# Scores of the short-range heads: even and odd heads in one step of 24 matmul instructions on four PSUM banks, alternating between the row halves of the array

## The reference

```python
def swa_sink_attention(q, k, v, positions, rel_bias, sinks):
    nb = S // BLOCK                                    # 256 // 128 = 2
    q = q.reshape(B, nb, BLOCK, SWA_KV_HEADS, SWA_GROUP, SWA_HEAD_DIM)     # 2 groups of 8 heads, 64 wide
    k_band = _band(k...); v_band = _band(v...)         # the block before and this block
    s = jnp.einsum('bnqhgd,bnkhd->bnhgqk', q, k_band).astype(jnp.float32) * (SWA_HEAD_DIM ** -0.5)
    s = s + bias                                       # relative bias of each head
    s = jnp.where(valid, s, -jnp.inf)                  # 0 <= distance < 128
    m = jnp.maximum(jnp.max(s, axis=-1, keepdims=True), sink)
    e = jnp.exp(s - m)
    p = e / (jnp.sum(e, axis=-1, keepdims=True) + jnp.exp(sink - m))
    out = jnp.einsum('bnhgqk,bnkhd->bnqhgd', p, v_band)
```

## Time and profile before

| | us |
|---|---|
| median of 3 runs | 2618.0 |
| lowest and highest | 2617.82, 2619.82 |
| profiled execution | 2617.56 |
| its span, first to last instruction | 2615.8 |
| PE busy | 2586.5 (99%) |
| DVE busy | 1652.0 (63%) |
| ACT busy | 1374.8 (53%) |

### The profile page before, as it was taken

How to read it: one execution, slowest core, us unless ns; L and a number is a source line. 1 busy time by engine, 2 the same in 40 slices (tenths; PEclk the granted TensorE clock), 3 DMA queues, 4 the chain that set the end, 5 groups by cost and what they waited for, 6 DMA issues and landing times.

```text
span 2615.8 us, 32927 instructions
## 1 busy us (share of the span) xinstructions
PE 2586.5 (99%) x13278; PEld 2179.5 (83%) x13278; DVE 1652.0 (63%) x2064; ACT 1374.8 (53%) x2013; POOL 0.2 (0%) x4
## 2 busy tenths in 40 slices
PE   9999999999999999999999999999999999999998
PEld 7877888888888888887888888888888888888887
DVE  7685566555655567568788866544566555655556
ACT  5664454444444446568878845544444444444444
POOL 0000000000000000000000000000000000000000
PEclk9999999999999999999999999999999999999999
DMA  6533565566556655555454437544565556555554
GB/s 224 165 134 137 195 208 193 193 192 187 189 189 193 193 190 168 190 178 176 137 179 145 131 128 249 164 158 138 184 206 186 188 193 193 193 188 190 189 190 145
DMA packets 235534, 468.78 MB, mean 179 GB/s; under 512 B 8219, under 2 KB 17654, under 8 KB 234102
## 3 DMA queue, kind: packets, MB, share of 16 engines
q1 hardware_dynamic: 234246, 465.11, 54.9%
q10 hardware_dynamic: 1136, 1.58, 0.2%
HBM read 460.36 MB, written 6.29 MB: 178 GB/s over the span
## 4 chain that ended last, share of the span: by engine, by line
PE 49%; DVE 1%; issue 0%; ACT 0%; DVEq 0%; ACTq 0%
PE ps L1176 10%; PE ps L1178 10%; PE ps L1177 10%; PE ps L1215 9%; PE ps L1214 5%; PE ps L1570 1%; PE ps L1583 1%; PE ps L1712 1%; PE ps L1687 1%; PE ps L1550 0%; PE ps L1233 0%; DVE AC L2965 0%; PE ps L1535 0%; PE ps L1609 0%; PE ps L1623 0%
## 5 line engine op out<-in xcount | busy, mean ns | idle before, releaser
L2483 DVE TENSOR_TENSOR WL<-Wt,WH 128x1024 fp32r<-128x1024 f32 (+1 forms) x861 | 1040.8, 1210 | 810.1 <-ACT WH L1767 750.1
L1767 ACT ACTIVATE WH<-Wt 128x1024 fp32r<-128x1024 f32 (+1 forms) x861 | 899.0, 1047 | 882.7 <-PE ps L1178 532.3
L1176 PE MATMUL ps<-WH,XT 128*128 128x512 f32 (+1 forms) x1184 | 472.1, 399 | 1.9 <-DVE Um L2875 1.6
L1176 PE MATMUL ps<-WH,HT 128*128 128x512 f32 (+2 forms) x1176 | 458.1, 390 | 4.5 <-DVE WL L2483 3.3
L1178 PE MATMUL ps<-WH,XT 128*128 128x512 f32 (+1 forms) x1184 | 459.5, 388 | 0.0
L1177 PE MATMUL ps<-WL,XT 128*128 128x512 f32 (+1 forms) x1184 | 458.6, 387 | 0.0
L1178 PE MATMUL ps<-WH,HT 128*128 128x512 f32 (+2 forms) x1176 | 451.7, 384 | 0.0
L1177 PE MATMUL ps<-WL,HT 128*128 128x512 f32 (+2 forms) x1176 | 451.2, 384 | 0.0
L1215 PE MATMUL ps<-XT,WH 128*128 128x512 f32 x960 | 336.5, 394 | 0.0
L1215 PE MATMUL ps<-HT,WH 128*128 128x512 f32 x960 | 336.5, 394 | 0.0
L1214 PE MATMUL ps<-XT,WL 128*128 128x256 f32 x960 | 266.6, 278 | 0.0
(11 more groups left out here) (390 smaller groups left out, 1965.8 us busy)
## 6 DMA issues: line engine op xcount, KB each, us to landing
Wt<-in_mlp_w SPq DMA_DIRECT2D x128, 1024.0 KB, 5.2
Wt<-in_w_up SPq DMA_DIRECT2D x64, 1024.0 KB, 5.5
Wt<-in_w_down SPq DMA_DIRECT2D x64, 1024.0 KB, 5.0
Wt<-in_w_in SPq DMA_DIRECT2D x53, 1024.0 KB, 5.1
Wt<-in_w_out SPq DMA_DIRECT2D x32, 1024.0 KB, 5.1
Wt<-in_xa_wk SPq DMA_DIRECT2D x16, 1024.0 KB, 5.1
Wt<-in_xa_wv SPq DMA_DIRECT2D x16, 1024.0 KB, 5.1
Wt<-in_xa_wq SPq DMA_DIRECT2D x16, 1024.0 KB, 5.1
```

What stands on the lines that cost most here:

```text
L1176: pe.matmul(o, xh, wh, start=start, stop=False)
L1767: act.activation(m.WH[:, i % NR, 0:2 * w], m.Wt[:, slot % NW, h * 2 * w:(h + 1) * 2 * w], ACT.Copy).then_inc(*up("wsplit.a", i))
L2483: dve.tensor_tensor(m.WL[:, i % NR, 0:2 * w], m.Wt[:, slot % NW, h * 2 * w:(h + 1) * 2 * w], m.WH[:, i % NR, 0:2 * w].bitcast(F32), SUB).t ...
```

## The change

The two scores steps of a group become one. It takes four banks from the queue at once and makes all 12 matmuls (24 instructions on PE), one for the even head and one for the odd head in turn, each pair on the two row halves and in different banks. One semaphore stands at their end. ACT then copies two banks instead of one. The mask steps of even and odd heads both come after the next half, with the first maximum. One `yield` less stands in each group, so each later step of a group comes one half earlier, and the next group of the same generator too: nine halves instead of ten. In `rope_products` a wait on the keys' transposition becomes one on the sums of the product before it.

```diff
-        def scores(hg, odd):
-            b = [p.bank(), p.bank()]
-            p.do("swa_scores", par, hg, odd, *b)
+        for hg in (par, par + 2):
+            b = [p.bank() for _ in range(4)]
+            p.do("swa_scores", par, hg, *b)
             p.free(b[0])
-            return b
-
-        for hg in (par, par + 2):
-            b = scores(hg, 0)
-            yield
-            p.do("swa_masked", par, hg, 0, b[1])
-            p.free(b[1])
-            b = scores(hg, 1)
-            yield
-            p.do("swa_masked", par, hg, 1, b[1])
-            p.free(b[1])
+            p.free(b[2])
+            yield
+            for odd in range(2):
+                p.do("swa_masked", par, hg, odd, b[2 * odd + 1])
+                p.free(b[2 * odd + 1])
             p.do("swa_largest", par, hg, 0)
             yield
             p.do("swa_largest", par, hg, 1)
...
     @named
-    def swa_scores(par, hg, odd, b0, b1):
-        k0, k1 = m.bank(b0), m.bank(b1)
+    def swa_scores(par, hg, *bs):
         g = hg // 2
         on.wait_ge(*at("swa.a", "keys"))
-        for s in freed(b0) + freed(b1):
-            on.wait_ge(*s)
+        for b in bs:
+            for s in freed(b):
+                on.wait_ge(*s)
         for i in range(2):
-            pb, tile = odd * 64, 2 * hg + i
+            tile = 2 * hg + i
             on.wait_ge(*at("swa.a", "queries", tile // 2))
-            q0 = m.QST[pb:pb + 64, tile, :]
-            kk = m.KTD[pb:pb + 64, g, :]
-            for o, qs, ks in ((k0[:, 2 * i * P:(2 * i + 1) * P], 0, 0),
-                              (k0[:, (2 * i + 1) * P:(2 * i + 2) * P], 1, 0),
-                              (k1[:, i * P:(i + 1) * P], 1, 1)):
-                t = pe.matmul(o, q0[:, qs * P:(qs + 1) * P], kk[:, ks * P:(ks + 1) * P], start=True, stop=True)
-        t.then_inc(*up(f"swa{par}.t", "scores", hg, odd))
+            for k, qs, ks in ((0, 0, 0), (0, 1, 0), (1, 1, 1)):
+                for odd in range(2):
+                    rows = slice(odd * 64, odd * 64 + 64)
+                    n = i if k else 2 * i + qs
+                    t = pe.matmul(m.bank(bs[2 * odd + k])[:, n * P:(n + 1) * P], m.QST[rows, tile, qs * P:(qs + 1) * P],
+                                  m.KTD[rows, g, ks * P:(ks + 1) * P], start=True, stop=True)
+        t.then_inc(*up(f"swa{par}.t", "scores", hg))
...
     @named
-    def swa_scores(par, hg, odd, b0, b1):
+    def swa_scores(par, hg, *bs):
         st = f"swa{par}"
-        on.wait_ge(*at(st + ".t", "scores", hg, odd))
+        on.wait_ge(*at(st + ".t", "scores", hg))
         swa_spare()
         if hg >= 2:
             on.wait_ge(*at(st + ".t", "turn", hg - 2, 1))
-        act.activation(m.S[:, par, odd, :, :, :].rearrange("p i b k -> p (i b k)"), m.bank(b0), ACT.Copy).then_inc(
-            *up(st + ".a", "scores", hg, odd, frees=b0))
+        for odd in range(2):
+            act.activation(m.S[:, par, odd, :, :, :].rearrange("p i b k -> p (i b k)"), m.bank(bs[2 * odd]), ACT.Copy
+                           ).then_inc(*up(st + ".a", "scores", hg, odd, frees=bs[2 * odd]))
...
-            on.wait_ge(*at("rope.v", "kt"))
+            on.wait_ge(*(at("rope.v", c - 1) if c else at("rope.v", "kt")))
```

## The result

| | before | after |
|---|---|---|
| median, us | 2618.0 | 2623.0 |
| profiled execution | 2617.56 | 2622.36 |
| its span | 2615.8 | 2620.6 |

The changed kernel takes 2622.95 us, the kernel before beside it on the same chip 2617.99, so 5.0 us more: ratio 1.0018, 95% interval 1.0011 to 1.0025. The forecast was +2.5.

What follows compares the result with a forecast made beforehand. PE was taken as the bound, with the chain through ACT and DVE already holding it up at three points. Scores -6.4 and waits +9.3 gave +2.9, taken as +2.5: 2618.0 + 2.5 = 2620.5 us, range 2611 to 2625.

Steps and rivals of the forecast that it cites:

- Scores: Short-range scores on PE: row halves overlap, four merged steps of 1.62 us replace eight, -6.4 us.
- Waits: PE's waits for the short-range chain after the steps move earlier: 14.0 us against 4.7, so +9.3 us.
- value 0: Group 0's value step, after half 40: PE waits 3.3 us for DVE to take out the turned probabilities.
- scores 2: Group 2's scores, after half 41: norm_turn took the only idle bank, four are wanted; PE waits 2.2 us.
- value 2: Group 2's value step, after half 49: DVE works without pause, turned probabilities come late; PE waits 3.3 us.
- DVE's idle time: Behind the PE wait at scores 2, through score copies and a split on ACT: DVE idle some 3.8 us.
- The clock: PE's granted clock in the short-range stretch: no wait of 1.6 us had lowered it; nothing in the sum.
- rival (d): Waits grow, or PE's clock falls after one (one half at 1.2 GHz costs 2.7): 2624 to 2626 us; chance 0.07.
- 200 to 203: Sign of being right: first matmul of w_out on XT starts at 200 to 203 us; account put it at 201.5.
- Rival (a): ACT and DVE keep up, 6.6 us of value waits and half the bank waits hidden: 2610 to 2612; chance 0.15.
- Rival (c): In the short-range stretch half of the waits go: -2 us, 2616; chance 0.11.
- Rival (b): Row halves don't overlap, merged scores step 2.95 us instead of 1.62: 2623.5, at most 2626; chance 0.13.

Runs made afterwards that it cites:

- run 1: Changed kernel with one more yield between turn and value of each group: 2616.59 us against 2618.79 for the kernel before.
- run 6: Kernel before with its steps moved as in the change, scores not merged, even step then odd step: 2623.82 us against 2618.22 for the kernel before.
- run 2: Changed kernel with three unread 512-column matmuls on PE ahead of values 0 and 2: 2619.92 us against 2618.79 for the kernel before.
- run 8: run 2 with two further unread matmuls ahead of scores 2: 2620.12 us against 2618.26 for the kernel before.
- run 12: run 9 with two unread matmuls ahead of turn 3: 2612.24 us against 2618.14 for the kernel before.
- run 3: Changed kernel with all 12 even-head instructions, then the 12 odd-head ones, in each scores step: 2627.38 us against 2618.79 for the kernel before.
- run 9: Changed kernel with a second written step table, exp and turn later, last two banks awaited before the last 8 instructions: 2613.81 us against 2618.26 before.
- run 7: Changed kernel with generators replaced by a written step table, last two banks awaited after 16 of 24 instructions: 2617.32 us against 2618.22 before.
- run 5: Kernel before, order unchanged, each odd scores step making one of its six matmuls (computation left out): 2616.28 us against 2618.22 for the kernel before.
- run 10: run 9 without alternation, twelve even-head then twelve odd-head instructions per scores step: 2613.36 us against 2618.14 for the kernel before.
- run 11: run 9 with scores 3 placed ahead of the exponentials of step 2: 2611.45 us against 2618.14 for the kernel before.

## Why the prediction came out as it did

**Scores: right.** The forecast took 1.62 us for a merged step, from the end of the half before, and a hundredth for the second half's later start; measured in the same way it is 1.63 us (109.97 + 0.23 to 111.82), and 7 ns. It rested on the column halves of the value step, and row halves behave alike when the heads alternate. The Trainium skill, "TensorE: Matmul & The Clock Gate", section "LDWEIGHTS", charges a load of 128 columns an estimated 107 ns; at that price 24 loads one after the other would take 2.6 us. The 24 instructions with their loads took 1.54 us, so the loads of the two row halves did not stand one after the other, which agrees with the Trainium skill, "TensorEngine Tiling (Array Packing)", section "Key Properties", that tiles load and multiply in parallel.

**Waits: right step by step.**

| PE waits ahead of | forecast, us | measured in after |
|---|---|---|
| scores 1 | 0.6 | 0.64 |
| turn 0 | 0.75 | 0.32 |
| value 0 | 3.3 | 3.31 |
| scores 2 | 2.2 | 2.07 |
| turn 1 | 1.65 | 1.50 |
| value 1 | 0.75 | 0.68 |
| scores 3 | 1.4 | 1.10 |
| turn 2 | 0.1 | none |
| value 2 | 3.3 | 3.14 |
| value 3 | 0 | none |
| sum | 14.0 | 12.76 |

All eight are at the steps named, each within 0.43 of its forecast. DVE's idle time behind the split that scores 2 holds up was put at 3.8 us; the timeline of DVE has it:

```profile
154.39 1.23 DVE L2478 TENSOR_TENSOR WL<-Wt,WH 128x1024 fp32r<-128x1024 f32 x1 [3.86 <-ACT WH L1761]
```

Runs 1 and 6 add whose waits they are: those at turn and value come from the moved steps, 3.1 us of those at scores from four banks at once. No half waits for its weights, and nothing is lost behind 204 us, both as forecast.

**The clock: wrong.** This is the term that failed, part of rival (d), which had 0.07. The forecast held that no wait of 1.6 us had lowered the clock, and its sum put nothing for waits twice as long, two of which it had itself forecast at 3.3 us. Runs 2, 8 and 12 price it: two stretches some 3 us, one 1.6. That is more than the whole difference between +2.5 and +5.0; without the clock the waits, 1.2 us smaller than forecast, would have given some +1.6 to +2. It is also why `w_out` began at 204.34 us, outside the 200 to 203 named. So the nearness of the total owes something to luck: two errors of opposite sign, 1.2 us too much for the waits and some 3 too little for the clock. Rival (d)'s own price for a single stretch, 2.7, was too high: the stretch is 3.41 us long, not a whole half at half speed.

**Rival (a)** (ACT and DVE keep up) fell with the waits in the table. **Rival (c)** too, at 12.76 us of waits. **Rival (b)** is refuted by run 3 beside after. The point from which (b) would have decided, a merged step of some 2.8 us, was not reached even by run 3's 2.62 (2.53 by the distance of starts), and yet that run is some 4 us slower than after. Four steps add 4.0 us and the waits give back 0.6 (12.18 for 12.76), with up to 1.7 of clock on top: in this order little swallows longer scores, since the bank waits ahead of scores 1 and 2 begin with PE's own `norm_turn` and move with it. In the order of run 9 nearly everything does.

**What stays open.** When a wait lowers the clock. In profiled executions it fell at the end of waits or up to 1.7 us behind them when they were 1.83 us long (run 1), 2.04 (run 7), 2.27 (runs 2 and 3), 2.28 (run 12), 2.33 (run 9), 2.71 (run 5) and more, and once behind one of 0.74 (run 6). It stayed up behind others of 2.07 (after), 2.29 (run 9), 2.32 (run 10), 2.84 (run 3), 3.31 and 3.13 (run 6). The kernel before has two groups of executions, 15 at 2617.4 to 2618.4 with a mean granted clock of 0.999 and 9 at 2619.0 to 2620.2 with 0.998; 1.5 us apart, they fit one stretch, which the profiled one does not have, so this was argued and not seen. Open too is what run 9's and run 11's orders would give with the scores steps of even and odd heads left apart; no run has that.

## What to carry to other kernels

A saving on the engine that bounds the kernel is only as good as the order around it. Here 6 us less of TensorE time came with +5.0 when a half was taken from the chain at the same time, and with -6.7 when the steps were placed so that VectorE and ScalarE were ready (run 11, same scores, two banks awaited later). The -6.7 is the order's doing more than the overlap's: run 10, in run 9's order and without the alternation, is as fast as run 9. Forecast the waits step by step, and then allow for the stretch of lower clock that may follow a wait of TensorE: here it followed waits from 1.83 us up (and once one of 0.74), not each of them, and cost 1.6 us where no later wait took it in. A wait that can't be removed can be filled with matmuls that nobody reads (runs 2 and 12; in run 8 a third filler brought nothing). Before a resource is taken four at a time, look who empties the last of them, and what stands ahead of that work in its engine's list.

## What the runs showed of the hardware

Two matmuls of 64 rows on different row halves run side by side in float32, weight loads too, starting 7 ns apart: 24 instructions in 1.54 us where 12 took 1.53. With the even heads' twelve ahead of the odd heads' twelve, the overlap covers only the last four instructions of the first set (run 3). The Trainium skill, "TensorE: Matmul & The Clock Gate", section "The mechanism", says that matmuls start in the order of the program. The traces disagree. In a value step each head has two instructions of 256 columns and then two of 128, yet the row at 144.19 us has four of 256 columns together: the second head's start ahead of the first head's shorter ones. And in run 3, by the spacing of starts, the thirteenth instruction in the list, the first for an odd head, starts at 111.54 us, when only nine of the first twelve have started.

The granted clock was 0.50 in stretches of 3.41 us or twice that (6.83 in runs 1 and 3), in some executions behind waits of no more than 1.8 to 2.3 us. The wait of 1.6 us in the kernel before, from which I had judged, says nothing on those. Of two kernels with a stretch each, run 9 loses 1.6 us by it and run 12 nothing, since a wait stood behind it.
